# Value products of two query blocks in the two column halves of TensorE, in an attention loop written out as 72 units

## The chip, the cores and the metric

The kernel runs on one core of a Trainium2 chip. TensorE (PE in the profile) multiplies matrices, and its weight loads (PEld) are listed apart; VectorE (DVE), ScalarE (ACT) and GpSimd (POOL) work on rows of numbers; SyncE (SP) issues transfers. Each engine runs its own list of instructions in order and waits for the others at semaphores. The metric is the device time of one execution in microseconds; lower is better.

## The reference

One step of a two-layer decoder over a prompt of 1040 positions (16 learned ones and 1024 of the prompt) and 64 sampled ones. The change is in the prompt attention of the even layer, 8 heads of 64:

```python
def fox_attend(q, c_q, pos_q, k, v, c_k, pos_k):
    s = jnp.einsum('bqhd,bkhd->bhqk', q, k).astype(jnp.float32) * (HEAD_DIM_B ** -0.5)
    bias = jnp.transpose(c_q, (0, 2, 1))[:, :, :, None] - jnp.transpose(c_k, (0, 2, 1))[:, :, None, :]
    mask = pos_k[None, :] <= pos_q[:, None]
    s = jnp.where(mask[None, None], s + bias, -jnp.inf)
    p = jax.nn.softmax(s, axis=-1)
    return jnp.einsum('bhqk,bkhd->bqhd', p.astype(v.dtype), v)
```

`c` is the running sum of log forget gates. Everything is float32.

## The kernel before

The kernel is one program, layer after layer: input projections and a convolution, the prompt attention (395 to 625 us of the profiled execution), the sample attention, the output projection, a feed-forward block, and then the odd layer. The matmuls outside the attention split float32 into a high and a low part (L665 to L667).

A **unit** of the prompt attention is one head and one block of 128 query rows. Block `i` (0 to 7) sees the first 128(i+1) keys; block 8 is the last 16 rows and sees all 1040. `att_units` (L314) lists them: an even head takes its blocks as 0, 1, ..., 8, an odd head as 0, 8, 1, ..., 7 (`ORDER`, L76). Below, "unit 6" is the unit with block 6.

A unit goes through these steps:
- **scores** on PE (L787): two matmuls for each 512 keys, a third that adds the causal mask, into banks 0 to 2 or 3 to 5 of the result memory `PS` in turn;
- **peak** on DVE (L1551): the row maximum, negated;
- **exp** on ACT (L1112) into `PB`, with the row sums in a second instruction, ACTIVATION_READ_ACCUMULATOR;
- **inverse** on DVE (L1557), and the scaling of `PB` by it on POOL (L552);
- **turning** on PE (L806): each 128 x 128 block of `PB` transposed into bank 5 or 6, four to a group; DVE copies the first group to `PT` (L1565), ACT the second (L1123);
- **values** on PE (L822): per key block one matmul with 64 columns of weights (the head's part of `VP`) and 128 columns of `PT`, all summed into partitions 0 to 63 of bank 7. Each of these float32 matmuls appears as two records, and each record has its weight load;
- **result** on ACT (L1125): bank 7 into `QKV`, over the queries.

Beside the units of one head, ACT (`head_high`, four steps, L1131) and DVE (`head_low`, three steps, L1571) prepare the operands of the next: `KS1`, `QS1`, `KS2`, `QS2`.

The order is written out by hand. At step `n` PE runs the scores of unit n, the turning of unit n-2 and the values of unit n-3. Each engine's loop does its part in the same steps. Scores of unit n wait for the exp of unit n-2 (two sets of score banks), values for the result of the unit before (one bank 7). `PB` has three buffers and `PT` two. The loop is a hardware loop of two passes (`Fori(0, 2)`), each of 4 heads or 36 units; the waits count from a register. At each pass's start SP loads the two value tiles of its four heads (`VP`, 0.5 MB each, L403 to L408), and ACT and DVE make the first head's operands, both after the last values of the pass before (`pv_done`).

Of the kernel before, what the change touches and what calls it, by code (L numbers as in the profile page):

```python
# [14 lines left out]
P = 128  # L15
# [60 lines left out]
ORDER = (tuple(range(9)), (0, 8, 1, 2, 3, 4, 5, 6, 7))  # L76

# [25 lines left out]
def build(nc, t):  # L103

    ctx = ExitStack()
    with ctx:
# [67 lines left out]
        PB, o = at("PB", o, [P, 3, TP])  # L174
        assert o >= stage_end
        VP, o = at("VP", o, [P, 2, NTT, P])
        PT, o = at("PT", o, [P, 2, NTT, P])
# [4 lines left out]
        ST4, o = at("ST4", o, [P, 3, 36])  # L182
        LFO, o = at("LFO", o, [P, NTT, NH])
        assert o <= B0

# [128 lines left out]
        def att_units():  # L314

            na = nb = 0
            for a in range(36):
# [7 lines left out]
        NA = ATT[-1][6] + 1 + (ATT[-1][3] == 8)  # L325
        NB = ATT[-1][7] + (ATT[-1][3] > 3)
# [29 lines left out]
        def _(sp):  # L356
# [46 lines left out]
            with sp.Fori(0, 2) as it:  # L403
                sp.wait_ge(pv_done, 1 + 36 * it)
                for j in range(2):
                    c = bass.ds((2 * it + j) * P, P)
                    sp.dma_start(VP[:, j, 0:8, :], vd[0:8 * P].rearrange("(b p) n -> p b n", p=P)[:, :, c]).then_inc(vp_ready[j], 16)
                    sp.dma_start(VP[0:META, j, 8, :], vd[8 * P:TP, c]).then_inc(vp_ready[j], 16)  # L408

            sp.wait_ge(s_ptb, 16)  # L410
            sp.wait_ge(att_evac, 1 + 72)
# [69 lines left out]
        def _(gp):  # L481
# [66 lines left out]
            with gp.Fori(0, 2) as it:  # L548
                for a, h2, j, i, m, n, _, _ in ATT:
                    gp.wait_ge(rc_ready, 36 * it + a + 1)  # L550
                    gp.nop(nofuse=True)
                    gp.tensor_scalar(PB[0:m, a % 3, 0:n], PB[0:m, a % 3, 0:n], ST4[0:m, 2, a:a + 1], 1.0,  # L552
                                     ALU.mult, ALU.mult).then_inc(pn_ready, 1)

            gp.wait_ge(att_evac, 1 + 72)
# [102 lines left out]
        def _(pe):  # L658
            pe.sem_inc(pv_done, 1)
# [127 lines left out]
            def scores(it, a, h2, j, i, m, n, na, nb):  # L787
                if a % 9 == 0:
                    pe.wait_ge(qk_hi, 16 * it + 4 * (a // 9) + 4)
                    pe.wait_ge(qk_lo, 12 * it + 3 * (a // 9) + 3)  # L790
                pe.wait_ge(exp_done, 36 * it + a + 1)
                if i == 8:
                    pe.nop(nofuse=True)
# [12 lines left out]
            def turn(it, a, h2, j, i, m, n, na, nb):  # L806

                pe.wait_ge(pn_ready, 36 * it + a + 1)
                for g in range((i + 4) // 4):
                    if g == 1:  # L810
                        pe.wait_ge(ptb_ready, NB * it + nb + 1)
                    else:
                        pe.wait_ge(pta_ready, NA * it + na + g // 2 + 1)
                    if i == 8:
                        pe.nop(nofuse=True)
                    for jt in range(4 * g, min(4 * g + 4, i + 1)):
                        kw = min(P, TP - jt * P)
                        mm = pe.transpose(PS[0:kw, 5 + g % 2, (jt - 4 * g) * P:(jt - 4 * g) * P + m], PB[0:m, a % 3, jt * P:jt * P + kw],  # L818
                                          IDN[0:m, 0:m])
                    mm.then_inc(tb_done if g == 1 else ta_done, 1)  # L820

            def values(it, a, h2, j, i, m, n, na, nb):  # L822
                if a % 18 == 0:
                    pe.wait_ge(vp_ready[j], 32 * it + 32)
                pe.wait_ge(pta_ready, NA * it + na + (2 if i == 8 else 1) + 1)
                if i > 3:
                    pe.wait_ge(ptb_ready, NB * it + nb + 2)
                pe.wait_ge(att_evac, 36 * it + a + 1)
                for jt in range(i + 1):
                    kw = min(P, TP - jt * P)  # L830
                    mm = pe.matmul(PS[0:HD, 7, 0:m], VP[0:kw, j, jt, HD * h2:HD * (h2 + 1)], PT[0:kw, a % 2, jt, 0:m],  # L831
                                   start=(jt == 0), stop=(jt == i))
                mm.then_inc(pv_done, 1)

            with pe.Fori(0, 2) as it:
                for n in range(36 + 3):
                    if n < 36:
                        scores(it, *ATT[n])
                    if 2 <= n < 38:
                        turn(it, *ATT[n - 2])  # L840
                    if n >= 3:
                        values(it, *ATT[n - 3])


            pe.wait_ge(att_evac, 1 + 72)
# [178 lines left out]
        def _(act):  # L1024
# [87 lines left out]
            def expo(it, a, h2, j, i, m, n, na, nb):  # L1112
                base = (0, 3)[a % 2]
                act.wait_ge(nm_ready, 36 * it + a + 1)
                src = PS[0:m, base:base + (n + 511) // 512, :].rearrange("p b n -> p (b n)")[:, 0:n]
                act.activation(PB[0:m, a % 3, 0:n], src, ACT.Exp, bias=ST4[0:m, 0, a:a + 1],
                               accum_out=ST4[0:m, 1, a:a + 1]).then_inc(exp_done, 1)

            def turned(it, a, h2, j, i, m, n, na, nb):
                if i > 3:  # L1120
                    act.wait_ge(tb_done, NB * it + nb + 1)
                    w = min(i + 1, 8) - 4
                    act.copy(PT[:, a % 2, 4:4 + w, 0:m], PS[:, 6, :].rearrange("p (k n) -> p k n", k=4)[:, 0:w, 0:m]).then_inc(ptb_ready, 1)  # L1123

            def result(it, a, h2, j, i, m, n, na, nb):  # L1125
                act.wait_ge(pv_done, 36 * it + a + 2)
                act.nop(nofuse=True)
                act.activation(QKV[HD * h2:HD * (h2 + 1), bass.ds(2 * it + j, 1), i * P:i * P + m].rearrange("p a n -> p (a n)"),
                               PS[0:HD, 7, 0:m], ACT.Copy).then_inc(att_evac, 1)

            def head_high(it, x, part):  # L1131

                h2 = x % 2
                if x >= 2 and part == 0:
                    act.wait_ge(qk_done, 36 * it + 9 * (x - 1))
                    act.nop(nofuse=True)
# [3 lines left out]
                src = QKV[own, bass.ds(2 * it + x // 2 + tile, 1), 0:TP].rearrange("p a n -> p (a n)")  # L1140
                act.activation(out, src, ACT.Copy, scale=scale).then_inc(qk_hi, 1)

            with act.Fori(0, 2) as it:
                act.wait_ge(pv_done, 1 + 36 * it)
                act.nop(nofuse=True)
                for part in range(4):
                    head_high(it, 0, part)
                for n in range(36 + 3):
                    if n < 36:
                        expo(it, *ATT[n])  # L1150
                    if 2 <= n < 38:
                        turned(it, *ATT[n - 2])
                    if n >= 3:
                        result(it, *ATT[n - 3])
                    if n < 27 and n % 9 in (2, 3, 4, 5):
                        head_high(it, n // 9 + 1, n % 9 - 2)
# [229 lines left out]
        def _(dve):  # L1386
# [164 lines left out]
            def peak(it, a, h2, j, i, m, n, na, nb):  # L1551
                base = (0, 3)[a % 2]
                dve.wait_ge(qk_done, 36 * it + a + 1)
# [3 lines left out]
            def inverse(it, a, h2, j, i, m, n, na, nb):  # L1557
                dve.wait_ge(exp_done, 36 * it + a + 3)
# [369 lines left out]
```

## Time and profile before

| | |
|---|---|
| median of 3 runs | 2953.59 us (2950.88 to 2954.36) |
| profiled execution, its own time | 2956.47 us |
| its span | 2954.8 us |
| TensorE busy | 2740.4 us, 93% |
| VectorE, ScalarE, GpSimd busy | 48%, 26%, 16% |
| mean granted TensorE clock | 0.939 of full speed |

The span is what the trace covers. A matmul is busy from its start to its modelled end, which overlaps with the next one's start, so starts are better marks than ends. "issue" as a releaser means that the engine waited for nothing the profile shows. The granted clock is 1.0 or 0.5 at any moment; a value between is a mean over the stretch. The attention takes 230 us of the 2955: 110 us for the first pass, 6.5 between the passes, 113 for the second.

### The profile page before, as it was taken

What the parts mean: (1) busy time and instruction counts of PE and PEld (TensorE: products, weight loads), DVE (VectorE), ACT (ScalarE), POOL (GpSimd) and SP (SyncE); (2) the same over time, 40 slices, a digit from 0 to 9 for tenths busy, and PEclk for the clock granted to TensorE, in tenths of its full rate; (3) what the DMA queues carried; (4) which work ended last, traced back from release to release, by engine and by line L of the source; (5) the groups of instructions that cost most, each with busy time, mean ns of one, the idle gap of its engine ahead of it and who ended that gap; (6) DMA issues with size and microseconds to landing.
All of it is one profiled execution on the core that took longest, in us unless ns stands there. A gap on an engine that the chain in (4) does not pass through costs nothing.

```text
span 2954.8 us, 37845 instructions
## 1 busy us (share of the span) xinstructions
PE 2740.4 (93%) x15813; PEld 2616.6 (89%) x15813; DVE 1408.4 (48%) x1943; ACT 755.8 (26%) x1256; POOL 486.4 (16%) x451
## 2 busy tenths in 40 slices
PE   6988778988899999999999989989999999999995
PEld 6988657766599999999999978989999999999994
DVE  2699955622157433333333574456633333333356
ACT  3100145533324211111111253123411111111133
POOL 3299932210013000000000031003100000000012
PEclk8998968877789999999999999999999999999998
DMA  6111120022131111111111232113211111111131
GB/s 200 45 31 29 43 80 15 0 91 100 43 118 58 44 43 44 44 48 49 47 44 44 74 104 77 43 52 114 69 45 43 44 43 43 44 49 44 44 93 61
DMA packets 217962, 173.18 MB, mean 59 GB/s; under 512 B 9170, under 2 KB 195650, under 8 KB 217801
## 3 DMA queue, kind: packets, MB, share of 16 engines
q1 hardware_dynamic: 211536, 159.35, 18.0%
q0 software_dynamic: 4960, 11.49, 1.3%
q8 instruction: 112, 1.84, 0.3%
q10 hardware_dynamic: 1320, 0.24, 0.1%
q14 instruction: 34, 0.27, 0.0%
HBM read 152.40 MB, written 18.93 MB: 58 GB/s over the span
## 4 chain that ended last, share of the span: by engine, by line
PE 82%; POOL 9%; DVE 3%; issue 3%; ACT 3%; DMA 1%; SPq 0%; ACTq 0%; DVEq 0%; POOLq 0%
PE PS L665 23%; PE PS L666 23%; PE PS L667 23%; POOL HF L538 4%; POOL S L537 3%; PE PS L831 3%; PE PS L887 2%; PE PS L799 1%; PE PS L818 1%; PE PS L803 1%; PE PS L679 1%; PE PS L869 1%; PE PS L680 1%; DMA RAW<-in_w_in_even 1%; DVE RSD L1654 1%
## 5 line engine op out<-in xcount | busy, mean ns | idle before, releaser
L665 PE MATMUL PS<-AH,WHI 128*128 128x368 f32 x3360 | 1129.2, 336 | 62.1 <-DVE QKV L1515 31.3
L666 PE MATMUL PS<-AL,WHI 128*128 128x368 f32 x3360 | 1122.4, 334 | 0.0
L667 PE MATMUL PS<-AH,WLO 128*128 128x368 f32 x3360 | 1118.0, 333 | 0.0
L665 PEld LDWEIGHTS PS<-AH,WHI 128*128 128x128 f32 x3360 | 641.8, 191 | 70.7 <-DVE QKV L1515 35.1
L666 PEld LDWEIGHTS PS<-AL,WHI 128*128 128x128 f32 x3360 | 640.9, 191 | 2.5 <-issue 0.5
L667 PEld LDWEIGHTS PS<-AH,WLO 128*128 128x128 f32 x3360 | 640.7, 191 | 0.0
L1719 DVE TENSOR_TENSOR HF<-S,PS 128x368 f32<-128x368 f32 x132 | 70.9, 537 | 678.3 <-ACT S L1054 678.3
L665 PE MATMUL PS<-HH,WHI 128*128 128x368 f32 x1056 | 353.6, 335 | 24.6 <-issue 16.7
L1039 ACT CAST WHI<-RAW 128x1024 fp32r<-128x1024 f32 x224 | 223.8, 1048 | 537.0 <-PE PS L667 531.0
L666 PE MATMUL PS<-HL,WHI 128*128 128x368 f32 x1056 | 352.9, 334 | 0.0
L667 PE MATMUL PS<-HH,WLO 128*128 128x368 f32 x1056 | 352.3, 334 | 0.0
L1732 DVE TENSOR_TENSOR Y<-Y,PS 128x368 f32<-128x368 f32 x480 | 251.0, 535 | 157.9 <-PE PS L667 157.9
L1402 DVE TENSOR_TENSOR WLO<-RAW,WHI 128x1024 fp32r<-128x1024 f32 x224 | 304.8, 1392 | 36.5 <-ACT WHI L1039 36.0
L1054 ACT ACTIVATE S<-PS 128x368 f32<-128x368 f32 x156 | 74.5, 477 | 885.2 <-PE PS L667 885.1
L601 POOL TENSOR_TENSOR YSM<-Y 128x736 f32<-128x736 f32 x12 | 21.3, 1777 | 1642.0 <-DVE Y L1732 1527.8
L665 PEld LDWEIGHTS PS<-HH,WHI 128*128 128x128 f32 x1056 | 201.5, 191 | 26.0 <-issue 17.2
L667 PEld LDWEIGHTS PS<-HH,WLO 128*128 128x128 f32 x1056 | 201.4, 191 | 0.0
L666 PEld LDWEIGHTS PS<-HL,WHI 128*128 128x128 f32 x1056 | 201.2, 190 | 0.2
L1486 DVE SCALAR_TENSOR_TENSOR CACC<-AEXT,PRT,CACC 128x1040 f32<-128x1040 f32 (+1 forms) x174 | 188.8, 1124 | 2.2
L538 POOL TENSOR_TENSOR HF<-HF,S 128x520 f32<-128x520 f32 x90 | 110.9, 1233 | 7.5
L1402 DVE TENSOR_TENSOR HL<-HF,HH 128x368 fp32r<-128x368 f32 x132 | 74.7, 566 | 74.8 <-ACT HH L1291 74.8
L537 POOL TENSOR_SCALAR S<-AEXT,PRT 128x520 f32<-128x520 f32 x90 | 100.2, 1113 | 8.9
(245 smaller groups left out, 2236.8 us busy)
## 6 DMA issues: line engine op xcount, KB each, us to landing
RAW<-in_w_ffn_gate SPq DMA_DIRECT2D x52, 512.0 KB, 3.9
RAW<-in_w_ffn_up SPq DMA_DIRECT2D x52, 512.0 KB, 4.8
RAW<-in_w_ffn_down SPq DMA_DIRECT2D x52, 512.0 KB, 3.6
RAW<-in_w_in_even SPq DMA_DIRECT2D x20, 512.0 KB, 4.8
Y<-x_spill SPq DMA_DIRECT2D x12, 736.0 KB, 8.0
RAW<-in_w_out_even SPq DMA_DIRECT2D x16, 512.0 KB, 4.8
KR<-in_cache_k SPq DMA_DIRECT2D x32, 256.0 KB, 3.1
VR<-in_cache_v SPq DMA_DIRECT2D x32, 256.0 KB
```

The source lines that it names most:

```text
L537: pool_op(gp.tensor_scalar(part, src(j), row(k, R_DW + j), 1.0, ALU.mult, ALU.mult))
L538: pool_op(gp.tensor_tensor(out, out, part, ALU.add))
L665: pe.matmul(out, wh, xh, start=first, stop=False)
L666: pe.matmul(out, wh, xl, start=False, stop=False)
L667: return pe.matmul(out, wl, xh, start=False, stop=last)
L831: mm = pe.matmul(PS[0:HD, 7, 0:m], VP[0:kw, j, jt, HD * h2:HD * (h2 + 1)], PT[0:kw, a % 2, jt, 0:m], start=(jt == 0), stop=(jt == i))
L1039: act.copy(WHI[:, pos + j, :], RAW[:, pos + j, :]).then_inc(w_hi, 1)
L1054: act.activation(s_tile[:, par, :] if bank0_to is None else bank0_to, PS[:, 2 * par, 0:C], func).then_inc(s_ready, 1)
L1402: return dve.tensor_tensor(out, x, f32(hi), ALU.subtract)
L1486: dve.scalar_tensor_tensor(acc, src, row(k, R_DW + j), acc, ALU.mult, ALU.add).then_inc(acc_step, 1)
L1719: dve.tensor_tensor(HF[:, u % 2, :], S[:, u % 2, :], PS[:, 2 * (u % 2) + 1, 0:C], ALU.mult).then_inc(gu_free, 1)
L1732: dve.tensor_tensor(y, y, PS[:, 4 + n % 3, 0:C], ALU.add).then_inc(d_free, 1)
```

## The change

- The two passes become one list of 72 units on every engine (`NU = 9 * NH`); the registers, branches and no-operations of the loop go. The next head's operands are prepared beside the units for heads 0 to 6 alike, so also for head 4.
- At every even step from 4 on, PE runs the values of units n-4 and n-3 as one block: key block by key block, first one unit's product, then the other's. The even-numbered unit goes to partitions 0 to 63 of bank 7, the other to 64 to 127. In the built program both kinds have tiles of 128 rows and 64 columns, as the products before had; the second kind is placed at column 64.
- ACT copies both results at the odd steps from 5 on.
- `PT` gets four buffers and moves to where `PB` was; `PB` gets four and moves over the four tiles of `QKV` that held v, which is in HBM by then.
- SP loads the value tile of each pair of heads once the products of the pair two before are done.

```diff
-            with sp.Fori(0, 2) as it:
-                sp.wait_ge(pv_done, 1 + 36 * it)
-                for j in range(2):
-                    c = bass.ds((2 * it + j) * P, P)
...
+            for j in range(NU // 18):
+                c = slice(j * P, (j + 1) * P)
+                if j >= 2:
+                    sp.wait_ge(pv_done, 18 * (j - 1))
+                sp.dma_start(VP[:, j % 2, 0:8, :], vd[0:8 * P].rearrange("(b p) n -> p b n", p=P)[:, :, c]).then_inc(vp_ready[j % 2], 16)
...
-            def values(it, a, h2, j, i, m, n, na, nb):
...
+            def values(first, second):
+
+                a, _, j, i, *_ = first
+                for u in (first, second):
+                    i, na, nb = u[3], u[6], u[7]
+                    if i > 3:
+                        pe.wait_ge(ptb_ready, nb + 2)
+                    pe.wait_ge(pta_ready, na + (2 if i == 8 else 1) + 1)
...
+                pe.wait_ge(att_evac, a + 1)
+                for jt in range(max(first[3], second[3]) + 1):
                     kw = min(P, TP - jt * P)
...
+                    for x, h2, _, i, m, *_ in (first, second):
+                        if jt <= i:
+                            out = PS[HD * (x % 2):HD * (x % 2 + 1), 7, 0:m]
+                            mm = pe.matmul(out, VP[0:kw, j % 2, jt, HD * h2:HD * (h2 + 1)], PT[0:kw, x % 4, jt, 0:m],
+                                           start=(jt == 0), stop=(jt == i))
+                mm.then_inc(pv_done, 2)
+
+            for n in range(NU + 4):
+                if n < NU:
+                    scores(*ATT[n])
+                if 2 <= n < NU + 2:
+                    turn(*ATT[n - 2])
+                if n >= 4 and n % 2 == 0:
+                    values(ATT[n - 4], ATT[n - 3])
...
+            for part in range(4):
+                head_high(0, part)
+            for n in range(NU + 5):
+                if n < NU:
+                    expo(*ATT[n])
+                if 2 <= n < NU + 2:
+                    turned(*ATT[n - 2])
+                if n >= 5 and n % 2 == 1:
+                    result(*ATT[n - 5])
+                    result(*ATT[n - 4])
+                if n < NU - 9 and n % 9 in (2, 3, 4, 5):
+                    head_high(n // 9 + 1, n % 9 - 2)
```

TensorE's order around the end of head 0, before (L818 is the turning, of unit 7 here; L831 the values of units 6 and 7; L799 and L803 with 16 rows the scores of head 1's unit 8; L801 adds the mask):

```order
L803 MATMUL PS<-KS_97,QS_93 128x128
L813 REGISTER_ALU
L818 MATMUL PS<-CST,PB 128x128 x4
L811 REGISTER_ALU
L818 MATMUL PS<-CST,PB 128x128 x4
L831 MATMUL PS<-PT,VP 64x128 x7
L791 REGISTER_ALU
L799 MATMUL PS<-KS_92,QS_91 16x512
```

The same place after (L812 is the turning, L832 the values, L795, L797 and L799 the scores):

```order
L799 MATMUL PS<-KS_96,QS_93 128x128
L812 MATMUL PS<-CST,PB 128x128 x8
L795 MATMUL PS<-KS_92,QS_91 16x512
L799 MATMUL PS<-KS_96,QS_93 16x512
L795 MATMUL PS<-KS_92,QS_91 16x512
L799 MATMUL PS<-KS_96,QS_93 16x512
L795 MATMUL PS<-KS_92,QS_91 16x16
L797 MATMUL PS<-MKR,IDR 16x16
L799 MATMUL PS<-KS_96,QS_93 16x16
L812 MATMUL PS<-CST,PB 128x16 x8
L812 MATMUL PS<-CST,PB 16x16
L832 MATMUL PS<-PT,VP 64x128 x15
```

The 7 products of unit 6 no longer stand between the turning of unit 7 and the scores of unit 8; they come behind that unit's turning, 15 products of units 6 and 7 together.

ScalarE's order at the loop's start, before (L1141 prepares the first head's operands, L1116 is the exp):

```order
L1143 UNCONDITIONAL_BRANCH
L1143 ISA
L1141 ISA
L1141 ACT_TABLE_LOAD
L1141 ACTIVATE KS_92<-QKV 64x1040
L1141 ISA
L1141 ACTIVATE QS_91<-QKV 64x1040
L1141 ACTIVATE KS_92<-QKV 64x1040
L1141 ACTIVATE QS_93<-QKV 64x1040
L1116 ACTIVATE PB,ST_101<-PS,ST_101 128x128
```

And after (L1137 prepares operands):

```order
L1137 ACTIVATE KS_92<-QKV 64x1040
L1137 ACTIVATE QS_91<-QKV 64x1040
L1137 ACTIVATE KS_92<-QKV 64x1040
L1137 ACTIVATE QS_93<-QKV 64x1040
L1116 ACT_TABLE_LOAD
L1116 ACTIVATE PB,ST_100<-PS,ST_100 128x128
```

The table load moves behind the four operand steps.

ScalarE's order at units 7 and 8 of an even head, before (L1123 copies turned weights, L1128 a result):

```order
L1116 ACTIVATE PB,ST_101<-PS,ST_101 128x1024
L1121 REGISTER_ALU
L1123 COPY PT<-PS 128x256
L1128 ISA
L1128 ACTIVATE QKV<-PS 64x128
L1114 REGISTER_ALU
L1116 ACTIVATE PB,ST_101<-PS,ST_101 16x1040
L1121 REGISTER_ALU
L1123 COPY PT<-PS 128x384
L1128 ISA
L1128 ACTIVATE QKV<-PS 64x128
```

The same units after (L1127 is the result):

```order
L1116 ACTIVATE PB,ST_100<-PS,ST_100 128x1024
L1123 COPY PT<-PS 128x256
L1127 COPY QKV<-PS 64x128 x2
L1116 ACTIVATE PB,ST_100<-PS,ST_100 16x1040
L1123 COPY PT<-PS 128x384
L1116 ACTIVATE PB,ST_100<-PS,ST_100 128x128
```

The results come two at a time, behind every second exp and its copy.

## Rows read from the trace of the kernel before

**Rows 1.** The chain of waits, 385 to 640 us: shares of the stretch by line.

```profile
by line: PE PS L831 36.2%; PE PS L799 15.8%; PE PS L818 15.7%; PE PS L803 11.7%; issue 5.7%; PE PS L801 2.5%; DMA KR<-in_cache_k 1.7%; PE PS L857 1.4%; DVE QS L1582 1.0%; PE PS L869 0.9%; ACT KS L1141 0.8%; SPq L415 0.8%; ACT QS L1141 0.8%;
```

**Rows 2.** Busy times by stretch: first pass, seam, second pass.

```profile
core 0: us, PE busy (x) PEld busy (x) DVE busy (x) ACT busy (x) POOL busy (x), PEclk, DMA share, GB/s
394.70:505.00 110.30, 106.59 (x696) 85.38 (x696) 60.91 (x121) 57.74 (x139) 28.30 (x36) 0.86 0.00 1
505.00:511.50 6.50, 0.00 (x0) 0.00 (x0) 3.14 (x3) 5.72 (x6) 0.00 (x0) 0.67 0.56 164
511.50:624.90 113.40, 109.28 (x697) 87.48 (x698) 61.10 (x121) 58.12 (x140) 28.31 (x36) 0.84 0.00 0
```

**Rows 3.** Timeline (start, duration, instruction): accumulator rows at ends of heads.

```profile
415.66 0.19 ACT L1116 ACTIVATION_READ_ACCUMULATOR PB<-PS,ST 16x1 f32 x1
...
446.10 0.19 ACT L1116 ACTIVATION_READ_ACCUMULATOR PB<-PS,ST 128x1 f32 x1
...
469.88 0.18 ACT L1116 ACTIVATION_READ_ACCUMULATOR PB<-PS,ST 16x1 f32 x1
...
470.95 0.19 ACT L1116 ACTIVATION_READ_ACCUMULATOR PB<-PS,ST 128x1 f32 x1
...
476.34 0.18 ACT L1116 ACTIVATION_READ_ACCUMULATOR PB<-PS,ST 16x1 f32 x1
...
497.20 0.19 ACT L1116 ACTIVATION_READ_ACCUMULATOR PB<-PS,ST 128x1 f32 x1
...
533.71 0.18 ACT L1116 ACTIVATION_READ_ACCUMULATOR PB<-PS,ST 16x1 f32 x1
```

**Rows 4.** Timeline, units 7 and 8 of head 2 on VectorE and ScalarE.

```profile
464.08 0.75 DVE L1584 TENSOR_SCALAR QS<-QBA,CST 32x1040 fp32r<-32x1040 f32 x1
...
464.95 1.20 DVE L1555 TENSOR_REDUCE ST<-PS 128x1 f32<-128x1024 f32 x1
...
466.19 1.11 ACT L1116 ACTIVATE PB<-PS,ST 128x1024 f32<-128x1024 f32 x1 [1.28 <-DVE ST L1555]
...
467.20 0.19 ACT L1116 ACTIVATION_READ_ACCUMULATOR PB<-PS,ST 128x1 f32 x1
...
467.42 0.16 DVE L1559 RECIPROCAL ST<-ST 128x1 f32<-128x1 f32 x1 [0.67 <-ACT PB L1116]
...
467.60 1.23 DVE L1555 TENSOR_REDUCE ST<-PS 16x1 f32<-16x1040 f32 x1
```

**Rows 5.** Timeline around head 3's first unit 8: value blocks (L831), what follows them.

```profile
471.16 1.50 PEld L831 LDWEIGHTS PS<-PT,VP 128*64 128x64 f32 x14 [0.17 <-issue]
...
472.83 0.40 PE L799 MATMUL PS<-KS,QS 128*16 128x512 f32 x1
...
474.05 1.23 DVE L1555 TENSOR_REDUCE ST<-PS 16x1 f32<-16x1040 f32 x1 [2.46 <-PE PS L803]
...
478.20 1.22 PEld L831 LDWEIGHTS PS<-PT,VP 128*64 128x64 f32 x18 [0.16 <-issue]
...
479.45 0.44 PE L799 MATMUL PS<-KS,QS 128*128 128x384 f32 x1
```

**Rows 6.** Timeline at both passes' starts: table loads, second pass's first scores.

```profile
388.91 1.28 ACT L1141 ACT_TABLE_LOAD   x1 [6.91 <-POOLq L545]
...
505.70 1.28 ACT L1141 ACT_TABLE_LOAD   x1 [0.34 <-issue]
...
511.55 0.47 PE L799 MATMUL PS<-KS,QS 128*128 128x128 f32 x1 [6.62 <-DVE QS L1584]
```

**Rows 7.** Groups by line, 394 to 626 us: results, copies of turned weights.

```profile
L1128 ACT ACTIVATE QKV<-PS 64x128 f32 x64 | 17.1, 267 | 29.6 <-PE PS L831 28.5
...
L1123 ACT COPY PT<-PS 128x512 f32<-128x512 f32 x8 | 4.7, 583 | 1.7 <-PE PS L818 1.2
```

**Rows 8.** Busy times by stretch, during the input projections; columns as in rows 2.

```profile
246.00:250.00 4.00, 2.95 (x18) 2.65 (x17) 4.00 (x4) 2.37 (x3) 3.75 (x4) 1.00 0.00 0
250.00:254.00 4.00, 4.00 (x26) 4.00 (x25) 3.93 (x6) 0.00 (x0) 3.78 (x3) 1.00 0.00 0
```

More of the change, by code:

```diff
@@ L76 @@
 ORDER = (tuple(range(9)), (0, 8, 1, 2, 3, 4, 5, 6, 7))
+NU = 9 * NH
 def constants():
@@ L316, in att_units @@
             na = nb = 0
-            for a in range(36):
+            for a in range(NU):
                 i = ORDER[(a // 9) % 2][a % 9]
@@ L545, in _ @@
             gp.sem_inc(ab_open, 1)
[L548 to L555, printed above, removed]
+            for a, h2, j, i, m, n, _, _ in ATT:
+                gp.wait_ge(rc_ready, a + 1)
+                gp.tensor_scalar(PB[0:m, a % 4, 0:n], PB[0:m, a % 4, 0:n], ST4[0:m, 2, a:a + 1], 1.0,
+                                 ALU.mult, ALU.mult).then_inc(pn_ready, 1)
+            gp.wait_ge(att_evac, 1 + NU)
             gp.wait_ge(lf_out, 16 * 3)
@@ L658, in _ @@
         def _(pe):
-            pe.sem_inc(pv_done, 1)
             pe.sem_inc(spv_done, 1)
@@ L835, in _ @@
[L835 to L845, printed above, removed]
+            def values(first, second):
[5 more added lines that the diff above has]
+                    pe.wait_ge(pta_ready, na + (2 if i == 8 else 1) + 1)
+                if a % 18 == 0:
+                    pe.wait_ge(vp_ready[j % 2], 32 * (j // 2) + 32)
+                pe.wait_ge(att_evac, a + 1)
+                for jt in range(max(first[3], second[3]) + 1):
+                    kw = min(P, TP - jt * P)
+                    for x, h2, _, i, m, *_ in (first, second):
[4 more added lines that the diff above has]
+                mm.then_inc(pv_done, 2)
@@ L1139, in head_high @@
                                     (0, QS2[0:HD, h2, :], HD ** -0.5))[part]
[L1140 to L1156, printed above, removed]
+                act.activation(out, QKV[own, x // 2 + tile, 0:TP], ACT.Copy, scale=scale).then_inc(qk_hi, 1)
+            for part in range(4):
[10 more added lines that the diff above has]
+                    head_high(n // 9 + 1, n % 9 - 2)
             act.wait_ge(cs_ready, 1)
@@ L1575, in head_low @@
                 if part == 0:
[L1576 to L1578 removed]
+                    dve.wait_ge(qk_hi, 4 * x + 1)
+                    low(KS2[0:HD, h2, :], QKV[own, x // 2 + HT, 0:TP], KS1[own, h2, :]).then_inc(qk_lo, 1)
                 elif part == 1:
[L1580 to L1597 removed]
+                    dve.wait_ge(qk_hi, 4 * x + 2)
+                    dve.scalar_tensor_tensor(QS1[other, h2, :], QKV[own, x // 2, 0:TP], HD ** -0.5, f32(QS1[own, h2, :]),
+                                             ALU.mult, ALU.subtract).then_inc(qk_lo, 1)
+                else:
+                    dve.tensor_scalar(QS2[64:96, h2, :], QBA[:], CST[0:32, K_MSK + x:K_MSK + x + 1], None, ALU.mult).then_inc(qk_lo, 1)
+            for part in range(3):
+                head_low(0, part)
+            for n in range(NU + 2):
+                if 1 <= n < NU + 1:
+                    inverse(*ATT[n - 1])
+                if n < NU:
+                    peak(*ATT[n])
+                if n >= 2:
+                    turned(*ATT[n - 2])
+                if n < NU - 9 and n % 9 in (4, 5, 6):
+                    head_low(n // 9 + 1, n % 9 - 4)
             dve.wait_ge(t_done, TU_LFS + 1)
```

110 lines of the change are left out of this document (37 added, 73 removed).

## Prediction

> **What bounds the kernel now.** First comes the chain of waits over the attention [rows 1]: 36% of that stretch stands on the value products (L831), 43% more on the score products and the turning (L799, L803, L818): TensorE's own work, in its own order. Then the busy times by stretch [rows 2]: in the two passes TensorE is busy 106.6 of 110.3 us and 109.3 of 113.4 us, VectorE 61 and ScalarE 58 in each. So TensorE bounds the loop, but not alone: the granted clock is 0.86 and 0.84, and as it has two levels (1.0 is 2.4 GHz, 0.5 is 1.2 GHz), about 31 and 36 us of the passes ran at the lower one. Between the passes lie 6.5 us without any matmul.
>
> Third, the timeline, read at one mark per unit: the start of the row that reads exp's accumulator. From head 1's last unit to head 2's last the marks lie 469.88 - 446.10 = 23.8 us apart, at the upper level; over an odd head 446.10 - 415.66 = 30.4 us and 497.20 - 469.88 = 27.3 us, with parts at the lower level; over head 4, which holds the seam, 533.71 - 497.20 = 36.5 us [rows 3]. Fourth, one unit close up [rows 4]: the exp starts when the peak ends, the inverse starts 0.03 us after the accumulator row ends, the next peak 0.02 us after the inverse. Peak, exp, inverse and the next peak are one chain through VectorE and ScalarE: 469.88 - 467.20 = 2.68 us from mark to mark for unit 8, and TensorE has no part in it. So in the large units a shorter product gains nothing; TensorE is late only around a change of head. There a unit 8 that follows a unit 0 has its mark 476.34 - 470.95 = 5.4 us later, and its peak waited 2.46 us for the scores [rows 3, 5].
>
> **The seam and the start.** Written out, head 4's operands are made beside head 3's units, as for heads 1 to 3. So 36.5 us become those of another even head, 23.8 us: -12.7. That holds the 6.6 us without a matmul [rows 6], the drain ahead of it and the refill at the lower level behind it. The loads of the value tiles for heads 4 and 5 now wait for the products of heads 0 and 1, those for 6 and 7 for heads 2 and 3: two heads ahead of their use, so nothing. At the start, the table load of 1.28 us that stood ahead of ScalarE's first copies [rows 6] now stands behind four of them, ahead of the first exp. The path to the first scores runs through those copies, so -1.2; the first exp waits for its scores about as long, so the load stays covered (if not, 0). At the end units 6 and 7 of the last head share a block: 2.3 us (below) and one wait of 0.6 in place of 1.7 and 1.9 us, -0.7; between 0 and -1.5.
>
> **The products in halves.** A value product of 128 columns is two records. Fourteen of them (unit 6) take 472.83 - 471.16 = 1.67 us, so 0.107 us each and 0.17 us for the drain that stands as "issue" at either end of a block [rows 5]. Two products, a couple, now cost 4 x 0.107 = 0.43 us. No row of before has a product in the upper half, so the couple is bounded: if the halves overlap wholly, 0.21 us; if a change of half drained the array as a change between turning and products does, 0.43 + 2 x 0.17 = 0.77 us. In between stands a row: unit 8's records have 16 columns, next to nothing to stream, and 18 of them take 479.45 - 478.20 = 1.25 us, 0.069 each [rows 5]. Such a record is a weight load and its issue, and these come one after another whatever the halves do. Four give 0.28 us, which I take.
>
> What is that worth on the path? A pair's block stands behind every second unit, twice as long and half as often. Over two heads 31 couples of full width arise, but those of units 0 to 3 run while VectorE and ScalarE are behind. On the path are the 5 + 7 of the pairs (4,5) and (6,7) of each head, which end around a change of head: 24 in two heads, some 90 in the eight (a few fall into the cold first head). Each 0.1 us on a couple is 9 us of the sum.
>
> **Step by step around a change of head, at the upper level.** Into an odd head: TensorE now runs the scores of unit 0, the turning of 7 and at once the scores of unit 8; the 1.67 us of unit 6's products between them are gone, and the 0.17 us of a drain with them, so unit 8's mark is 1.8 us earlier. They come back with unit 7's: (6,7) takes 7 x 0.28 + 0.21 + 0.17 = 2.3 us where unit 7 alone took 1.9: +0.4. Unit 2's scores no longer stand behind the first unit 8's narrow products (1.25 us, of which some 0.8 showed past the chain); unit 3's now do, and these have unit 0's with them (+1.3); the pair (4,5) ahead of unit 0 adds 0.3. Sum -0.6 us an odd head, four of them: -2.4. Into an even head: pair (4,5) 1.8 us and (6,7) 2.3 us stand in two units instead of 1.5, 1.7 and 1.9 us in three; that would give 1 us, but a wait is added that takes it: nothing.
>
> The wait: a pair's products need both results of the pair before evacuated, and these two copies (0.27 us each) now stand on ScalarE behind the next unit's exp and its copy of turned weights (up to 0.58 us) [rows 7]. So a block begins no sooner than some 1.1 us after an exp, and behind it on TensorE queue the next unit's scores, for which VectorE's peak waits. Between units 4 and 7 of a head the preparation of the next head keeps VectorE behind anyway: its last step there starts at 464.08 and takes 0.75 us, and the next peak starts at 464.95 with only the inverse between [rows 4]. Around a change of head the wait leaves TensorE idle about 1 us at each of two blocks. Its bounds: nothing, if exp is ahead; 2 us more a head, 16 in all, if every block met it.
>
> The register instructions ahead of the waits go, which ran while their engines waited, and the added buffers of P and of turned weights take away no wait, since the order on TensorE keeps the same distance: nothing.
>
> **Sum.** -12.7 - 1.2 - 0.7 - 2.4 = -17 us, all in the attention; what follows starts from its last result and moves up with it. The profiled execution took 2956.5 us (span 2954.8), 2.9 above the median, so 2939.5 on its own scale and 2953.6 - 17 = 2937 us against the median.
>
> **What the Trainium skill says.** The Trainium skill, "TensorEngine Tiling (Array Packing)", Theoretical Speedup and Key Properties, gives column halves up to twice the rate and lets different tiles load and multiply in parallel; no run here shows it. By it the couple would be the 0.21 us of the second rival. The Trainium skill, "TensorE: Matmul & The Clock Gate", Part 3 (The mechanism), speaks against the change: a weight load passes a running matmul only where the row groups differ, and both halves here use all 128 rows. The trace does not agree as far as it goes: the 14 loads of one block lie within 1.50 us, beside their matmuls, in one and the same group [rows 5].
>
> **Rivals.**
> The halves do not overlap: 0.43 us a couple, 90 x 0.15 = +13.5, so 2950 us. For it: fp32 products are two records each, and only the second of one can run beside the first of the next. Against: nothing in the order forces it.
>
> Whole overlap: 90 x 0.07 = -6: 2931 us. Against: the 0.069 us a record.
>
> Loads do not pass: a couple is 4 x 0.069 + 2 x 0.107 = 0.49 us, +19: 2956 us. Against: the row of loads above.
>
> Slower: every change of half drains. 0.77 us a couple, 90 x 0.49 = +44, so 2981 us, at every pair of units from 4 to 7. It decides from 0.28 + 17/90 = 0.47 us a couple. For it: a change of tile shows 0.17 us at each block's start. Against: the tile's size stays, only its place changes.
>
> The clock: TensorE idles more (its 216 us busy in the passes are 182 at the upper level, 46 for two heads, and 31 x 0.15 less is 41, in some 47), and the lower level lasts longer. For it: the lower stretches in the passes [rows 2]. Against: earlier the level held while TensorE was busy 2.95 of 4 us, and through the next 4 [rows 8]. At the lower level two heads need 82 us for 47, so each us there costs 0.42; as much again as now less the seam's ten, 57 us, is +24: 2961 us. It eats the gain from 40 us on.
>
> **How the numbers follow.** Forecast 0.50, whole overlap 0.13, no overlap 0.15, loads not passing 0.05, draining 0.11, clock 0.06. Less than 0.2% (5.9 us) a measurement of this kernel does not tell from no change, so faster is below 2947.7 and slower above 2959.5. Faster: nearly all of the first two, a third of the third, a little of the rest: 0.68. Same: half of the third and fourth, rests of the others: 0.15. Slower: draining, half of the clock case, edges: 0.17. The likeliest case alone spans 2927 to 2948 us (couple 0.25 to 0.35 us, wait 0 to 1 us a head more, the ends 1 or 2). The range of 8 in 10 goes from 2920 to 2968 us: it leaves out most of the draining case and little else.
>
> **What would show it.** Right: no stretch without matmuls inside the attention, marks of head 4 some 24 us apart; a block of (6,7), 30 records, near 2.3 us at the upper level; peaks of the large units no closer than before; TensorE idle ahead of blocks on ScalarE's result. Wrong: that block at 3.4 us (no overlap) or near 5.8 (draining); more than 60 us at 0.5 in the stretch; even heads well under 23 us, which would mean that TensorE, not the chain of peak and exp, set them.

## The result, and the profile after

The changed kernel took 2922.36 us (median of 4 runs, 2919.21 to 2923.12), the kernel before 2952.24 beside it: ratio 0.9892, 95% interval 0.988 to 0.9905. The forecast was 2937 us (-17); the gain was about 30, inside the range of 2920 to 2968 but nearly twice the size. The profiled execution took 2923.12 us with a span of 2921.4, 33.4 less than before; the attention's last result is copied by 589.9 us in place of 624.8.

The chain of waits from 385 to 590 us, by line; L832 are the value products now, L1549 the peak, L795 and L799 scores, L812 the turning:

```profile
by line: PE PS L832 23.5%; DVE ST L1549 16.7%; PE PS L795 10.5%; PE PS L812 9.7%; PE PS L799 8.8%; ACT PB L1116 8.2%; DVE PT L1559 5.1%; DVE QS L1574 3.0%; DVE KS L1396 2.4%; issue 2.3%; PE PS L797 1.9%; DVE QS L1577 1.8%; DVE ST L1553 1.8%
```

Against [rows 1], where value products held 36% and VectorE next to nothing, the chain now goes through VectorE and ScalarE for over a third.

The busy times head by head, heads 1 to 7, from the end of one head's last accumulator row to the end of the next one's [rows 3 are starts of these rows]; columns as in [rows 2]. Before:

```profile
415.85:446.29 30.44, 29.21 (x188) 23.82 (x187) 15.75 (x32) 15.32 (x37) 7.09 (x9) 0.78 0.01 2
446.29:470.06 23.77, 23.62 (x166) 18.46 (x163) 16.16 (x30) 15.52 (x38) 7.05 (x9) 1.00 0.01 2
470.06:497.39 27.33, 26.08 (x186) 21.06 (x185) 12.71 (x29) 11.29 (x34) 7.09 (x9) 0.88 0.00 1
497.39:533.90 36.51, 28.93 (x166) 22.99 (x165) 19.63 (x33) 21.43 (x43) 7.08 (x9) 0.77 0.10 29
533.90:562.65 28.75, 27.52 (x188) 22.42 (x187) 15.75 (x32) 15.34 (x37) 7.09 (x9) 0.82 0.00 0
562.65:586.43 23.78, 23.64 (x165) 18.48 (x163) 16.15 (x30) 15.53 (x37) 7.05 (x9) 1.00 0.00 0
586.43:616.84 30.41, 29.16 (x186) 23.56 (x184) 12.71 (x29) 11.26 (x33) 7.09 (x9) 0.78 0.00 0
```

After:

```profile
413.78:439.23 25.45, 22.74 (x179) 19.31 (x178) 15.45 (x32) 14.59 (x37) 7.12 (x9) 0.80 0.01 2
439.23:462.06 22.83, 19.54 (x173) 15.27 (x172) 15.97 (x30) 16.04 (x38) 7.11 (x9) 1.00 0.09 24
462.06:486.67 24.61, 21.41 (x179) 17.97 (x178) 15.44 (x32) 14.60 (x37) 7.12 (x9) 0.86 0.01 2
486.67:509.51 22.84, 19.57 (x173) 15.27 (x172) 15.97 (x30) 16.04 (x38) 7.11 (x9) 1.00 0.08 24
509.51:536.44 26.93, 24.25 (x179) 20.58 (x178) 15.54 (x32) 14.59 (x37) 7.12 (x9) 0.75 0.00 1
536.44:559.28 22.84, 19.57 (x173) 15.27 (x172) 15.98 (x30) 16.05 (x39) 7.11 (x9) 1.00 0.00 1
559.28:582.44 23.16, 19.67 (x176) 16.27 (x175) 12.51 (x29) 10.73 (x33) 7.11 (x9) 0.93 0.01 1
```

First, head 4's seam is gone: 36.51 to 22.84. Second, an even head held the upper level in both and is 0.94 us shorter, with TensorE busy 19.5 us of 22.8 where it was busy 23.6 of 23.8. Third, the four odd heads fell from 116.9 to 100.2 us, 16.8 where the forecast had 2.4. Apart from the seam's head they are the ones with a clock below 1.00. The time at the lower level is 2 x (1 - clock) x length: 44 us in the odd heads before, 34 after.

The block of units 6 and 7, 30 records, in the timeline of head 2:

```profile
444.53 1.97 PE L832 MATMUL PS<-PT,VP 128*64 128x128 f32 x30 [0.63 <-DVE PT L1559]
...
446.42 0.50 PE L795 MATMUL PS<-KS,QS 128*128 128x512 f32 x1
```

Unit 7's 16 records alone, in head 2 of the kernel before:

```profile
475.68 1.94 PE L831 MATMUL PS<-PT,VP 128*64 128x128 f32 x16
```

So the 14 records of unit 6 add next to nothing to the 16 of unit 7. The next scores start 1.89 us after the block's first record.

What TensorE waited for in the attention, 388 to 590 us (in total, times, longest):

```profile
PE PS L812 <- DVE PT L1559: 17.0, 29, 1.3
PE PS L795 <- DVE QS L1577: 16.2, 1, 16.2
PE PS L832 <- ACT QKV L1127: 3.2, 6, 1.3
PE PS L832 <- DVE PT L1559: 1.9, 3, 0.6
```

The wait of 16.2 us is the one ahead of the first scores. The added wait for results shows 3.2 us in the whole attention, in six places.

### The profile page after: what moved, and what is told of

Same layout as the page of the kernel before. It is cut to its first block, busy times and chain, and to the rows that moved or that the text cites. A ratio compares the mean times of both kernels' runs of the same rounds, so it can differ in the third digit from the quotient of the medians.

```text
span 2921.4 us, 37015 instructions
## 1 busy us (share of the span) xinstructions
PE 2690.0 (92%) x15813; PEld 2576.9 (88%) x15813; DVE 1405.4 (48%) x1943; ACT 754.1 (26%) x1255; POOL 486.3 (17%) x451
## 4 chain that ended last, share of the span: by engine, by line
PE 79%; POOL 9%; DVE 5%; ACT 3%; issue 2%; DMA 1%; SPq 0%; ACTq 0%; DVEq 0%; POOLq 0%
PE PS L663 23%; PE PS L664 23%; PE PS L665 23%; POOL S L538 4%; POOL HF L539 3%; PE PS L887 2%; PE PS L832 2%; DVE ST L1549 1%; PE PS L869 1%; PE PS L677 1%; PE PS L678 1%; PE PS L795 1%; PE PS L812 1%; DMA RAW<-in_w_in_even 1%; PE PS L799 1%
## 5 line engine op out<-in xcount | busy, mean ns | idle before, releaser
L663 PE MATMUL PS<-HH,WHI 128*128 128x368 f32 x1056 | 353.6, 335 | 24.6 <-issue 16.7
L538 POOL TENSOR_SCALAR S<-AEXT,PRT 128x520 f32<-128x520 f32 x90 | 112.6, 1251 | 8.9
L539 POOL TENSOR_TENSOR HF<-HF,S 128x520 f32<-128x520 f32 x90 | 98.6, 1095 | 7.5
```

The lines of the kernel that those rows point to most:

```text
L538: pool_op(gp.tensor_scalar(part, src(j), row(k, R_DW + j), 1.0, ALU.mult, ALU.mult))
L539: pool_op(gp.tensor_tensor(out, out, part, ALU.add))
L663: pe.matmul(out, wh, xh, start=first, stop=False)
```

## The experiments

Theory A: the products side by side made what the forecast missed. Rival B: the pairs as such did. Later, theory E: much of it was the lower clock level in the odd heads.

**The loop written out alone**: values(n-3) at each step, all in the lower half, a result after each.

```diff
-                if n >= 4 and n % 2 == 0:
-                    values(ATT[n - 4], ATT[n - 3])
+                if n >= 3:
+                    values(ATT[n - 3])
```

> The loop written out as 72 units, but the value products of one unit at a time in the lower column half, as before, and a result after each: the seam and the start alone. Theory A (the products' overlap made what the forecast missed): head 4 falls from 36.5 to 23.8 us, the other heads keep their lengths (even 23.8, odd 27 to 30), -12.7 -1.2, so 2938 us, ratio 0.9953. Rival B (the pairs as such, their order and fewer drains, made it): the same 2938 here. Rival C (writing the loop out saves more than the seam, by the register instructions that go): every head shorter, 2926 us or less, ratio 0.991.

Measured 2935.06 us, ratio 0.993 (0.9918 to 0.9942): by the medians 17 of the 30 us are the written-out loop's, 13 the pairs'. Head 4 took 23.77 us: the seam is worth 12.7, as forecast. Rival C is out: even heads stay at 23.8. The odd heads took 110.2 us, 6.7 less than before, with 31 us of the lower level; neither theory had said that.

**A pair's products one unit after the other**, the pairs kept:

```diff
-                for jt in range(max(first[3], second[3]) + 1):
...
-                    for x, h2, _, i, m, *_ in (first, second):
-                        if jt <= i:
+                for x, h2, _, i, m, *_ in (first, second):
+                    for jt in range(i + 1):
```

> The changed kernel with the products of a pair one unit after the other (all of the first, then all of the second), still in the two column halves: pairs, order, waits and buffers as changed, only no two products side by side. Theory A: TensorE has its 83 us of value products back (46.5 in the changed kernel), even heads go from 22.8 back to 23.7 us, odd ones by 2 us and more each, so 2936 us, ratio 0.9945 (2934 to 2940). Rival B: block (6,7) takes 3.2 us in place of 2.0 but the heads stay within 0.5 us of the changed kernel's: 2922 to 2926 us, ratio 0.990 to 0.991.

Measured 2946.99 us, ratio 0.9971 (0.9954 to 0.9989), 11 above theory A's figure. The overlap is worth 24.6 us by the medians, and without it the pairs are slower than single products by 12. Rival B is out. How much of the 24.6 is the products' own time is less sure: three of the eleven executions took 2932 us at a mean granted clock of 0.949, the other eight 2942 to 2952 at 0.939 to 0.944. The same block of units 6 and 7 in this kernel:

```profile
447.43 3.08 PE L832 MATMUL PS<-PT,VP 128*64 128x128 f32 x30 [0.63 <-DVE PT L1559]
...
450.44 0.50 PE L795 MATMUL PS<-KS,QS 128*128 128x512 f32 x1
```

One microsecond inside the block, value products alone (length, matmul records, weight loads), changed kernel first:

```profile
444.90:445.90 1.00, 1.00 (x24) 1.00 (x22) 1.00 0.09 16
```

```profile
449.10:450.10 1.00, 1.00 (x12) 1.00 (x10) 1.00 0.00 0
```

In series the records start 0.109 us apart, which is 0.44 us for a couple. Side by side each half starts one every 0.109 us, which is 0.22 us for a couple: the halves overlap wholly. The series is not strict: where the block changes from one half to the other, the last three records of the first half and the first ones of the second start in turn (nine weight loads between 448.50 and 449.00 us, five between 447.60 and 448.10). Even heads took 24.6 us, 1.8 longer. That is what their two blocks are longer by, from first record to the next scores: 3.01 - 1.89 us for (6,7) and 2.14 - 1.46 for (4,5). The odd heads took 118.0 us, with 51 us of the lower level.

**The peak ahead of the inverse** of the unit before, on VectorE:

```diff
-                if 1 <= n < NU + 1:
-                    inverse(*ATT[n - 1])
                 if n < NU:
                     peak(*ATT[n])
+                if 1 <= n < NU + 1:
+                    inverse(*ATT[n - 1])
```

> The changed kernel with one swap on VectorE: the peak of unit n stands ahead of the inverse of unit n-1, so that the peak runs beside the exp of the unit before instead of behind it. Theory A (after the change the chain of peak, exp, inverse and next peak sets the even heads, 22.8 us, and TensorE's 19.6 us busy do not): even heads fall to 20 to 20.5 us, odd ones by 1 to 2, in all -16 us against the changed kernel: 2906 us, ratio 0.9843. Rival (waits around the blocks set them, the results' wait above all): within 2 us of the changed kernel, 2922. Against it: the inverse now stands behind a peak of up to 1.1 us, and GpSimd's scaling and the turning behind it, which could give +8 us: 2930.

Measured 2920.77 us, 0.9887 (0.9873 to 0.9902): no difference from the changed kernel. Even heads fell by 0.5 us only, and an odd head at the upper level took 24.72. TensorE's waits in this kernel:

```profile
PE PS L812 <- POOL PB L551: 24.8, 27, 1.8
```

The chain of peak and exp was broken and another took its place: the later inverse holds up GpSimd's scaling, and the turning waits for that (in the changed kernel it waited for VectorE's copies).

**Unit 8 of the odd heads later**:

```diff
-ORDER = (tuple(range(9)), (0, 8, 1, 2, 3, 4, 5, 6, 7))
+ORDER = (tuple(range(9)), (0, 1, 2, 3, 4, 8, 5, 6, 7))
```

> The changed kernel with the odd heads' order 0,1,2,3,4,8,5,6,7 in place of 0,8,1 to 7: the unit of 16 query rows no longer stands among the small units behind the even head's own unit 8. Theory A (the lower clock level in the odd heads, 34 us of it in the changed kernel, comes from the stretch of units 8,0,8,1,2 where TensorE has little to do, and each us there costs 0.37): the lower time in the odd heads falls below 10 us, -9 us: 2913 us, ratio 0.9868. Rival (the level falls at each odd head whatever the order, or its time is hidden): within 2 us of the changed kernel, 2922, ratio 0.9892.

Measured 2922.08 us, 0.989 (0.9875 to 0.9904), with 30 us at the lower level in the odd heads. The theory was wrong: less than 10 us did not come. What moved is the place: the level now falls in units 3 to 7, where it fell in units 2 and 3.

**Results ahead of the next exp** on ScalarE:

```diff
+                if n >= 5 and n % 2 == 1:
+                    result(*ATT[n - 5])
+                    result(*ATT[n - 4])
                 if n < NU:
                     expo(*ATT[n])
```

> The changed kernel with one move on ScalarE: the two results of a pair stand ahead of the next unit's exp and not behind it and its copy of turned weights. The forecast's step on the added wait (a block begins no sooner than 1.1 us after an exp, TensorE idle 1 us at two blocks of a head): 16 us of idle go, 10 us or more on the path, 2912 us or less, ratio 0.986. Rival (the trace of the changed kernel: the blocks waited for results 3.2 us in all, 6 times): 0 to -3 us, 2919 to 2922, ratio 0.9885; above 2922 if the copies, 0.54 us a pair, now hold up the exp.

Measured 2920.54 us, 0.9889 (0.9872 to 0.9905): no difference in the time, as the rival said. The profiled execution took 2911.0 us, the other three 2920.4 to 2921.0. In this profile the blocks wait for no result any more, an even head takes 22.15 us (0.7 less), and two odd heads held the level throughout. An even head and one of these two:

```profile
435.53:457.68 22.15, 19.51 (x174) 15.23 (x172) 15.89 (x30) 15.63 (x37) 7.05 (x9) 1.00 0.09 25
457.68:480.18 22.50, 18.43 (x179) 15.36 (x177) 15.22 (x32) 15.07 (x38) 7.08 (x9) 1.00 0.01 2
```

**A filler that holds the clock**: matmuls whose result is overwritten.

```diff
+                if (a // 9) % 2 and a % 9 in (1, 2, 3):
+                    for _ in range(2):
+                        pe.matmul(PS[:, base, :], QS1[:, h2, 0:P], KS1[:, h2, 0:512], start=True, stop=True)
```

> The changed kernel with two matmuls of 512 columns more ahead of the scores of units 8, 1 and 2 of each odd head, into the bank that these scores overwrite: work that computes nothing, in the stretch before the clock falls. Theory A (the lower level in the odd heads, 34 us in the changed kernel, is entered because TensorE has little to do there, and costs 0.42 us in each): the level holds, -14 us, less up to 5 us for 24 matmuls at 0.22: 2913 us, ratio 0.986. Rival (the level falls whatever stands there, or its time is hidden behind other engines): 0 to +5 us, 2922 to 2928, with 30 us or more of the odd heads still at 0.5.

Measured 2916.22 us, 0.9871 (0.9854 to 0.9887). The lower level in the odd heads went from 34 to 3 us, and they took 94.8 in place of 100.2 us with 24 matmuls more. The time is 6 us below the changed kernel's, with intervals that overlap. An odd and an even head:

```profile
412.74:436.46 23.72, 19.97 (x185) 16.51 (x184) 15.33 (x32) 14.59 (x37) 7.09 (x9) 1.00 0.01 2
436.46:459.29 22.83, 19.55 (x173) 15.29 (x172) 15.96 (x30) 16.04 (x39) 7.08 (x9) 1.00 0.08 24
```

So work on TensorE ahead of the fall does keep the level up, though not in every head (14 us of the lower level in the last profile below).

**The preparation of the next head earlier**: VectorE's three steps ahead of peaks that wait for scores, ScalarE's first two moved up (not shown); and the same with the peak first in units 4 to 7.

```diff
+                h, r = divmod(n, 9)
+                if n < NU - 9:
+                    for part, pos in enumerate((2, 4, 4) if h % 2 else (1, 3, 3)):
+                        if pos == r:
+                            head_low(h + 1, part)
```

> The changed kernel with the next head's preparation moved: VectorE's first step ahead of the peak of the second unit of an even head (third of an odd one), its two others ahead of the fourth (fifth), where VectorE waits 1.5 to 2.2 us for scores; ScalarE's first two steps by one to three units earlier. Theory D (in units 4 to 7 VectorE is what sets the pace after the change, with 3.2 us of preparation a head between its peaks): 1 to 2 us off each of seven heads: 2911 us (2908 to 2915), ratio 0.9855. Rival (TensorE or the chain over ScalarE sets them, the preparation is hidden): within 2 us of 2922, ratio 0.9892; later if ScalarE's steps now hold up an exp.

> The kernel before it (preparation moved) and for units 4 to 7 also the peak ahead of the inverse of the unit before. Theory D and A together (with VectorE free, the chain of peak, exp and inverse is the next bound of the large units, TensorE the one behind it): a further 0.5 to 1 us a head: 2904 us, ratio 0.983. Rival (the later inverse holds up GpSimd's scaling and TensorE's turning by as much as the chain gives): the same as that kernel.

Measured 2918.11 us, 0.9878 (0.9861 to 0.9894), and 2922.01, 0.9889 (0.9873 to 0.9906): the first between theory D's 2908 to 2915 and the rival's 2 us around 2922, the second without the gain that it forecast, neither clear of the changed kernel. In the first, units 4 to 8 of an even head took 12.4 us in place of 13.25, but units 0 to 3 took 10.5 in place of 9.6: a moved step of ScalarE now stands ahead of the first exp, whose unit took 2.40 us in place of 1.31. The head stayed at 22.94.

**Both useful edits together**, and a filler ahead of the first scores as well:

```diff
+            for _ in range(26):
+                pe.matmul(PS[:, 0, 0:P], IDN, IDN, start=True, stop=True)
```

> The changed kernel with both edits that helped: the results of a pair ahead of the next exp, and the two idle matmuls ahead of the scores of units 8, 1 and 2 of an odd head. By the two profiles: even heads 22.15 us, odd ones 22.5 plus 0.9 for the filler, all at the upper level: heads 1 to 7 together 159.5 us in place of 168.7, -9: 2913 us, ratio 0.986. Rival (the filler and the earlier results use up the same idle time, or the level falls all the same): no better than the filler alone, 2916, ratio 0.987.

> The first kernel of these four, and 26 idle products of 128 columns in the 16 us in which TensorE waits ahead of the first scores, where the level has fallen before every kernel's first head (14 us of it). Theory E: the level is up at the first scores or shortly behind them, 8 us less of it at 0.3 each: -2.5: 2910.5 us, ratio 0.9852. Rival (units 0 to 4 of the first head hang on VectorE and ScalarE, or the level falls again): the same as without, 2913; above it if the filler runs past the operands at 394.

Measured 2910.89 us, 0.9865 (0.9843 to 0.9886), and 2913.14, 0.9874 (0.9854 to 0.9895): the first near its forecast, the second at its rival's figure. The second had 10 us less of the lower level in head 0 and the wait ahead of it, yet units 1 to 4 of head 0 kept their lengths to 0.1 us: at the start TensorE is not what is late.

**The filler without the overlap, and with single products:**

> The kernel with a pair's products one unit after the other, with the filler as well, so that the clock holds. It tells how the 24.6 us that the overlap was worth fall apart. Theory E (1.8 us a head, 14.3 us, are the products' own time on TensorE at the upper level; the other 10 came from the lower level, which lasted 17 us longer without the overlap): this kernel stands 14 us above the changed kernel with filler: 2931 us, ratio 0.992. Rival (all of it is the products' time, the clock only goes along): 24 us above it, 2941, ratio 0.9955.

> The loop written out with single products, with the same filler, so that the clock holds. Theory E (what the forecast missed in the odd heads was half the lower level): odd heads 25 us in place of 25.7 to 28.7, -9: 2926 us, ratio 0.9905, so that pairs and halves together are worth some 10 us at a level that holds, in place of the 13 measured between the two kernels without filler. Rival (the filler only adds its own time to a TensorE that is busy throughout): 2935 to 2940, ratio 0.994 or more.

Measured 2941.02 us, 0.9963 (0.9951 to 0.9975), and 2936.62, 0.9943 (0.9925 to 0.9961). By the times both rivals hold. The heads at the upper level say more. An odd and an even one, serial pairs first, single products below:

```profile
465.91:492.17 26.26, 22.95 (x190) 18.95 (x188) 15.45 (x32) 14.59 (x37) 7.08 (x9) 1.00 0.01 2
492.17:516.78 24.61, 21.36 (x169) 17.50 (x167) 15.98 (x30) 16.02 (x38) 7.08 (x9) 1.00 0.08 23
```

```profile
415.68:441.61 25.93, 24.82 (x194) 20.13 (x193) 15.44 (x32) 15.27 (x37) 7.08 (x9) 1.00 0.01 2
441.61:465.38 23.77, 23.62 (x166) 18.48 (x163) 16.15 (x30) 15.42 (x37) 7.05 (x9) 1.00 0.08 23
```

With the level held the overlap is worth 26.26 - 23.72 = 2.5 us an odd and 1.8 an even head, 15.5 over heads 1 to 7, near theory E's 14; between the medians lie 25. What the other 9 us are, profiles of one execution each don't show: the two spans differ by 22, 3 of them behind the attention. With single products the filler itself costs 1.5 us an odd head (0.55, 0.47 and 0.46 in units 8, 1 and 2), since TensorE is busy there, and that eats what the level gives.

**Changed kernel, best version, before and loop written out, once more:**

> The changed kernel once more, for its lower-level time in the odd heads (34 us in the first profile) and its time beside the best version on one chip. Theory E (the level falls in each odd head by a rhythm of its own, so that its time differs from execution to execution): between 20 and 45 us, heads that hold the level throughout at 22.8 us, 0.27 us for each us at the lower level; 2922 us within 3. Rival (the halves keep the level up by themselves): 34 us within 4 again.

> Results ahead of the exp, and the filler, once more beside the changed kernel: 2911 us, 9 to 12 below it, if what the profiles showed (even heads 22.15 in place of 22.83, odd ones 23.5 in place of some 25) is the edits' doing; within 3 us of it if the first run was a lucky one.

> The kernel before once more, for the lower-level time of its odd heads (44 us in the first profile). Theory E: between 30 and 55 us, and the odd heads' length is 24.4 us plus 0.43 for each us of it, so that the 9.7 us that the lower level gave between the two kernels is partly its price (0.43 against 0.27 each) and partly chance. Rival: 44 us within 4.

> The loop written out with single products once more, for the lower-level time of its odd heads (31 us in the first profile, 44 in the kernel before). Theory E: 25 to 50 us, 0.40 to 0.43 us for each. Rival (writing the loop out takes 13 us of it away): 31 us within 4.

Measured 2920.66 us, 0.9894 (0.987 to 0.9918); 2912.78, 0.9858 (0.9831 to 0.9886); 2954.45, 1.0001 (0.9982 to 1.0019); 2935.05, 0.9937 (0.992 to 0.9955). The best version is 8 us below the changed kernel here, 11 in the first runs. The intervals overlap, but here each of its five executions lies below each of the changed kernel's six. The lower level of the odd heads: changed 24 us (34 in the first profile), before 41 (44), written out 31 (31), best version 14 (3), 10 of them in its last head. Only the changed kernel tells theory E from its rival: there it varies, with one head that held the level; odd heads 1, 3 and 5:

```profile
413.34:438.81 25.47, 22.74 (x179) 19.31 (x178) 15.44 (x32) 14.59 (x37) 7.11 (x9) 0.80 0.01 2
...
461.65:484.45 22.80, 18.61 (x179) 15.45 (x178) 15.34 (x32) 14.59 (x37) 7.11 (x9) 1.00 0.01 2
...
507.31:530.45 23.14, 19.92 (x179) 16.65 (x178) 15.44 (x32) 14.59 (x36) 7.12 (x9) 0.93 0.01 1
```

The best version's last head, where the filler did not hold the level:

```profile
550.54:576.83 26.29, 23.75 (x182) 19.92 (x180) 12.51 (x29) 11.37 (x34) 7.12 (x9) 0.81 0.01 2
```

## Why the prediction was too small

| term of the sum | forecast | measured (means of two profiles of each kernel) |
|---|---|---|
| seam, head 4 | -12.7 | -12.7 (36.5 to 23.8, loop written out alone) |
| start and head 0 | -1.2 | -2.6 (its last row ends at 413.6, not 416.1) |
| odd heads, at the upper level | -2.4 | -7.0 (97.8 to 90.8 for the four) |
| odd heads, the lower level | 0 | -10.7 (18.4 to 7.7) |
| heads 2, 4, 6 beside the seam | 0 | -2.8 (23.77 to 22.84 each) |
| end | -0.7 | -0.6 (last exp to last result, 8.0 to 7.4) |

The measured terms sum to 36. The last result ended 35 and 38 us earlier, the spans differ by 33 and 36, the medians by 30 and 34. The 97.8 are 4 x 24.45: units 0 to 3 of the written-out loop and 4 to 7 of the same with filler, all at the upper level. The 90.8 are 3 x 22.80, the odd head above, and 22.3 for the last head, which prepares nothing (its 23.26 with filler, less 0.92). The lower level's part is the rest: 116.9 and 115.4 us less 97.8 before, 100.2 and 96.8 less 90.8 after.

**The step that failed is "Step by step around a change of head, at the upper level"**: it reckons the heads at the upper level alone, finds -0.6 us for an odd head and nothing for an even one, and lets the lower level's cost stand. Measured, the odd heads gave 7.0 us at the upper level and 10.7 at the lower, the even ones 2.8. Split the other way, by the medians of both sets of runs, the pairs in halves gave 13 to 14 us where the forecast had 2.4 + 0.7, and the written-out loop 17 to 19 where it had 12.7 + 1.2.

*The lower level.* It cost 0.43 us for each of its microseconds before (18.4 of 43), as the clock rival had said (0.42), but 0.27 after (7.7 of 29). At the upper level TensorE now works 18.6 of an odd head's 22.8 us, so there is idle time that a slower clock can use up first; no run tests this reading by itself. And there was less of it: 43 us before, 31 in the written-out loop, 29 after (means of two profiles; the changed kernel's were 34 and 24). The clock rival expected more idle time to lengthen it, and that did not come. Most of the fall in time came with writing out the loop, the fall in price with the pairs in halves (0.40 in the written-out loop, 12.4 of 31 us). Why writing out the loop shortens it, no run shows.

*The odd heads at the upper level.* Unit by unit, from mark to mark (us):

| unit | 0 | 8 | 1 | 2 | 3 | 4 | 5 to 7 |
|---|---|---|---|---|---|---|---|
| single products, written out | 1.07 | 5.36 | 2.62 | 2.26 | 2.34 | 2.66 | 8.13 |
| changed | 1.11 | 3.60 | 2.73 | 2.10 | 2.55 | 2.37 | 8.34 |
| forecast of the difference | +0.3 | -1.8 | +0.4 | -0.8 | +1.3 | 0 | 0 |

The main term stood: -1.76 in unit 8. The terms that were to give it back were mis-sized: +0.04, +0.11 and +0.21 in units 0, 1 and 3 against +0.3, +0.4 and +1.3. In unit 2 only 0.16 of 0.8 came. The +0.3 and +0.4 were the price of longer blocks: (6,7) was taken at 2.3 us and took 1.9, as long as unit 7 alone before.

*The even heads.* "A wait is added that takes it: nothing" was wrong in size. Without the wait an even head takes 22.15 us, so the pairs give 1.6 and not 1, and the wait takes 0.7 and not all. Its 2 us of idle a head, 16 in all, were 3.2.

*The couple.* It was taken at 0.28 us and measured 0.22, the size of the whole-overlap rival (0.21), though that rival's 2931 us lie 9 above the measured time. The reason given for 0.28, that weight loads come one after another at 0.069 us each whatever the halves do, failed twice: the loads of both halves together start 0.055 us apart on average, and the 0.069 had one drain of 0.17 us in it (without that, 18 narrow records in 1.08 us are 0.060 each). Nor did the no-overlap rival's reason hold, that only neighbouring records of two products can run side by side: both halves start records throughout.

*What held.* Two blocks a head on the path were right for the even heads: what the blocks lose in series, the head loses. The no-overlap rival said 2950; the kernel in series took 2947. In the large units a shorter product gained nothing: units 6 and 7 of an even head take 3.15 and 2.81 us in both kernels. The drain at each change of half is out: the block took 1.97 us, not 5.8.

On the Trainium skill, "TensorEngine Tiling (Array Packing)", Theoretical Speedup: of its factor of up to two for column halves these products get all, 0.44 / 0.22 = 2.0. The Trainium skill, "TensorE: Matmul & The Clock Gate", Part 3 (The mechanism), lets a load overlap a running matmul only where the row groups differ. Both halves use all 128 rows here, and 0.49 us a couple, the sum by it, is more than twice what was measured; here the measurement decides. The same section lets a load go ahead into a background weight buffer too; no run here tells whether that is at work.

## What to carry to other kernels

Work out a gain apart for stretches at the upper and the lower clock level: less work on TensorE pays where the clock is low, and the idle time it leaves makes the low level itself cheaper (0.43 to 0.27 us for each of its microseconds here). Look for the few units after which the level falls; a little idle work ahead of them can be worth more than it costs where TensorE waits there anyway, and not where it is busy. Pairing two products paid only where they ran side by side: as a pair in series the same blocks were slower than single ones (an even head 24.6 us against 23.8).

## What the hardware showed that was not expected

Two float32 products of 64 columns in the two column halves, alternating, took 0.22 us a couple against 0.44 in series, with all 128 rows used by both. Apart from head 0 and the seam, the level fell inside the attention only in odd heads, between their unit of 16 query rows and unit 4 (with that unit moved back, in units 3 to 7). Yet with the same busy time there (2.71 of 3.60 us in unit 8, 1.61 of 2.10 in unit 2) one head of the changed kernel held it, and two others in the same execution did not. What decides between them stays open. Six matmuls more in each odd head, for 0.9 us a head, left 3 us of the lower level in three profiles of kernels with the halves and 14 in a fourth; the changed kernel had 34 and 24.
